# The odd table's rows loaded behind the last scatter, and the fifth tile's even rows added by a transfer, in a decoder layer with a mixture of experts

## The reference, cut to what matters

```
for each block of up to 128 routed rows of one expert:
    h = x[token rows];  y = (silu(h @ wg[e]) * (h @ wu[e])) @ wd[e]
routed[token] += y * gate                     # each token has 6 experts of 64
shared = (silu(x @ sh_wg) * (x @ sh_wu)) @ sh_wd
r = ALPHA * x + routed + shared
out = (r - mean(r)) * rsqrt(var(r) + eps) * g2 + b2
```

## Time and profile before

| | |
|---|---|
| time, median of three runs | 2006.88 us (2005.97 to 2007.66) |
| the profiled execution's own time | 2021.99 us |
| its span | 2019.8 us |
| TensorE busy | 1963.6 us, 97% of the span |
| VectorE, ScalarE, GpSimd busy | 67%, 46%, 30% |
| mean granted clock of TensorE | 0.988 of full speed |
| HBM read and written | 338.58 MB and 81.84 MB |

### The profile page before, as it was taken

One profiled execution on the slowest core, in us unless ns is written; L12 is line 12 of the kernel. 1 busy time (PEld: TensorE's weight loads), 2 busy tenths in 40 slices (PEclk: granted clock), 3 DMA queues, 4 the chain that ended last, 5 costly groups with the idle time before them and its releaser, 6 DMA issues. The chain is left out here.

```text
span 2019.8 us, 32329 instructions
## 1 busy us (share of the span) xinstructions
PE 1963.6 (97%) x9421; PEld 1479.3 (73%) x9422; DVE 1345.5 (67%) x2558; ACT 926.4 (46%) x1615; POOL 613.9 (30%) x403
## 2 busy tenths in 40 slices
PE   8999999999999999999999889999999999999996
PEld 7887787877768766668878637777777777777772
DVE  2794643444206677779867738887777877778876
ACT  2111221234212244550044237777777777677764
POOL 2433232323322220002143533333333333233331
PEclk9999999999999999989999899999999999999998
DMA  6122312132532210047671567999999999999986
GB/s 204 42 68 89 104 42 63 43 86 63 124 93 84 79 59 27 26 156 263 218 283 43 188 242 230 312 373 346 323 342 338 341 326 346 327 314 330 342 280 177
DMA packets 170898, 390.66 MB, mean 193 GB/s; under 512 B 27936, under 2 KB 100929, under 8 KB 146112
## 3 DMA queue, kind: packets, MB, share of 16 engines
q1 hardware_dynamic: 132032, 302.71, 41.5%
q0 software_dynamic: 29568, 70.09, 13.9%
q10 hardware_dynamic: 9216, 16.78, 2.2%
HBM read 338.58 MB, written 81.84 MB: 208 GB/s over the span
## 5 line engine op out<-in xcount | busy, mean ns | idle before, releaser
L660 PE MATMUL a_bank<-x_hi,w_hi 128*128 128x512 f32 x928 | 376.8, 406 | 0.0
L660 PE MATMUL a_bank<-x_hi,w_lo 128*128 128x512 f32 x928 | 363.4, 392 | 0.0
L660 PE MATMUL a_bank<-x_lo,w_hi 128*128 128x512 f32 x928 | 362.2, 390 | 0.0
L2382 DVE TENSOR_TENSOR u_lo<-w_gu,u_hi 128x1024 fp32r<-128x1024 f32 x225 | 268.4, 1221 | 37.0 <-ACT u_hi L2024 29.2
L2024 ACT ACTIVATE u_hi<-w_gu 128x1024 fp32r x225 | 230.5, 1065 | 17.5 <-SPq L1511 16.7
L594 POOL CAST w_hi<-w_raw 128x1024 fp32r<-128x1024 f32 x56 | 65.2, 1164 | 557.2 <-PE a_bank L660 557.2
L2397 DVE TENSOR_TENSOR d_lo<-w_d,d_hi 128x1024 fp32r<-128x1024 f32 x150 | 177.2, 1222 | 82.5 <-ACT d_hi L2132 81.4
L1814 PE MATMUL e_bank<-u_hi,x_g_hi 128*128 128x512 f32 x450 | 208.4, 463 | 0.0
L660 PEld LDWEIGHTS a_bank<-x_hi,w_hi 128*128 128x128 f32 x928 | 174.9, 188 | 39.4 <-issue 6.1
L660 PEld LDWEIGHTS a_bank<-x_hi,w_lo 128*128 128x128 f32 x928 | 174.5, 188 | 38.1
L660 PEld LDWEIGHTS a_bank<-x_lo,w_hi 128*128 128x128 f32 x928 | 175.3, 189 | 32.5 <-issue 0.5
(11 more groups left out here) (397 smaller groups left out, 3676.2 us busy)
## 6 DMA issues: line engine op xcount, KB each, us to landing
w_gu<-in_moe_wg SPq DMA_DIRECT2D x64, 1024.0 KB
w_gu<-in_moe_wu SPq DMA_DIRECT2D x64, 1024.0 KB
w_d<-in_moe_wd SPq DMA_DIRECT2D x64, 1024.0 KB, 25.5
w_raw<-in_w_in SPq DMA_DIRECT2D x53, 512.0 KB, 3.8
gates<-gate_out ACTq DMA_DIRECT2D x64, 256.0 KB, 2.0
g_sb<-gates SPq DMA_DIRECT2D x16, 1024.0 KB, 5.3
acc_odd<-zero POOLq DMA_DIRECT2D x9, 512.0 KB, 15.2
work<-in_w_out SPq DMA_DIRECT2D x4, 1024.0 KB, 7.8
```

The lines of the kernel that those rows point to most:

```text
L660: ins = pe.matmul(bank[h][:, :], w[:, c % 2, k, :], x[:, k, cols], start=(k == 0 and j == 0), stop=(k == KD - 1 and j == 2))
L2382: dve.tensor_tensor(up_part(u_lo[j]), up_weights(slot, j), up_part(u_hi[j]).bitcast(F32), ALU.subtract).then_inc(u_lo_dve, 1)
```

## The change

All odd blocks now go to `acc_odd`, block 2n-1 too; even blocks and the very last one, 2n+1, go to `acc`. `odd_whole` is given when block 2n-1 has landed, and by its place in POOL's stream only behind the issue of the last scatter. So all eight loads of odd rows stand behind that issue; three (tiles 4, 0, 5) before `rows_landed`, the others between the even rows, in the order in which the tail uses them. Tile 4's even rows are added by a POOL transfer like those of tiles 5 to 7 (order: 5, 4, 6, 7). VectorE's `total(4)` falls away; ScalarE makes tile 4's row sum and mean (`sum_of_four`). VectorE's `inverse(2, 4)` moves ahead of tile 5's sum, tile 5's sum ahead of tile 4's centering, and `center(6)` ahead of `inverse(4, 6)`.

```diff
@@ -1466,8 +1466,11 @@
         def odd_row(t):
             return x1_n[:, t, :] if t < NU else row_out(t)
 
-        def even_row(t):
-            return row_out(t) if t < NU else x1_n[:, t, :]
+        def summed_row(t):
+            return row_out(t) if t == NU else x1_n[:, t, :]
+
+        def normed_row(t):
+            return x1_n[:, t, :] if t == NU else row_out(t)
 
         DOWN_BANK = {NU: 2, NU + 1: 4, NU + 2: 2, NU + 3: 0}
 
...
@@ -1597,20 +1600,30 @@
                     sp.dma_start(tail_d, d['sh_wd'][0].rearrange('(k p) n -> p k n', p=P)).then_inc(tail_in, 16)
                     sp.dma_start(g2, d['ln2_g'].broadcast_to([P, D])).then_inc(ln_in2, 16)
                     sp.dma_start(b2, d['ln2_b'].broadcast_to([P, D])).then_inc(ln_in2, 16)
+            def odd_rows(t):
+                sp.dma_start(odd_row(t), acc_odd[t * P:(t + 1) * P, :]).then_inc(odd_in[t], 16)
+
+            def even_rows(t):
+                sp.dma_start(row_out(t), acc[t * P:(t + 1) * P, :]).then_inc(acc_row_in[t], 16)
             sp.wait_ge(odd_whole, 1)
             sp.wait_ge(d_blocks, blocks_until(E - 3) + 2)
-            for t in range(NU, NT):
-                sp.dma_start(odd_row(t), acc_odd[t * P:(t + 1) * P, :]).then_inc(odd_in[t], 16)
+            odd_rows(NU)
             sp.wait_ge(gu_blocks, blocks_until(E - 2) + 2)
-            for t in range(NU):
-                sp.dma_start(odd_row(t), acc_odd[t * P:(t + 1) * P, :]).then_inc(odd_in[t], 16)
+            odd_rows(0)
+            odd_rows(5)
             sp.wait_ge(gu_blocks, 2 * n + 4)
             sp.wait_ge(rows_landed, 1)
-            for t in range(NU + 1):
-                sp.dma_start(even_row(t), acc[t * P:(t + 1) * P, :]).then_inc(acc_row_in[t], 16)
+            even_rows(0)
+            odd_rows(1)
+            even_rows(1)
+            odd_rows(6)
+            for t in range(2, NU):
+                odd_rows(t)
+                even_rows(t)
+            odd_rows(7)
             for i, t in enumerate((0, 1, 4, 5, 6)):
                 sp.wait_ge(finished, i + 1)
-                sp.dma_start(out[0, t * P:(t + 1) * P, :], row_out(t)).then_inc(out_stored, 16)
+                sp.dma_start(out[0, t * P:(t + 1) * P, :], normed_row(t)).then_inc(out_stored, 16)
             for h in range(2):
                 cols = slice(h * HALF, (h + 1) * HALF)
                 sp.wait_ge(finished, h + 6)
...
@@ -1680,29 +1693,21 @@
             pool.wait_ge(acc_rest, 16 * (NT - NU))
             n = trips(pool)
 
-            def body(b, s, i, ahead=True, table=None, whole=False):
+            def body(b, s, i, ahead=True):
                 if ahead:
                     gather(s, b + 4)
-                if whole:
-                    pool.wait_ge(scattered[1], 16 * i + 16)
-                    pool.sem_inc(odd_whole, 1)
                 pool.wait_ge(y_act, b + 2)
                 pool.wait_ge(so_ready, b + 2)
                 pool.wait_ge(scattered[s], 16 * i + 16)
-                if table is not None:
-                    pool.wait_ge(scattered[1 - s], 16 * i + 32 - 16 * (1 - s))
                 pool.sem_inc(gathers, 1)
-                pool.indirect_dma_start(out=((acc, acc_odd)[s] if table is None else table)[:, :], out_offset=bass.IndirectOffsetOnAxis(ap=idx_out[:, s:s + 1], axis=0),
+                pool.indirect_dma_start(out=(acc, acc_odd)[s][:, :], out_offset=bass.IndirectOffsetOnAxis(ap=idx_out[:, s:s + 1], axis=0),
                                         in_=y_out[:, s, :], in_offset=None, bounds_check=S - 1, oob_is_err=False,
                                         compute_op=ALU.add
                                         ).then_inc(scattered[s], 16)
-            last = n - 1
-            with pool.Fori(0, last) as i:
+            with pool.Fori(0, n) as i:
                 for s in range(2):
                     body(2 * i + s, s, i)
-            body(2 * last, 0, last, whole=True)
-            body(2 * last + 1, 1, last, table=acc)
-            body(2 * n, 0, n, ahead=False, table=acc)
+            body(2 * n, 0, n, ahead=False)
             pool.wait_ge(y_act, 2 * n + 3)
             pool.wait_ge(so_ready, 2 * n + 3)
             pool.wait_ge(scattered[0], 16 * n + 32)
@@ -1710,16 +1715,19 @@
             pool.indirect_dma_start(out=acc[:, :], out_offset=bass.IndirectOffsetOnAxis(ap=idx_out[:, 1:2], axis=0),
                                     in_=y_out[:, 1, :], in_offset=None, bounds_check=S - 1, oob_is_err=False,
                                     compute_op=ALU.add).then_inc(scattered[0], 16)
+            pool.wait_ge(scattered[1], 16 * n + 16)
+            pool.sem_inc(odd_whole, 1)
             pool.wait_ge(scattered[0], 16 * n + 48)
-            pool.wait_ge(scattered[1], 16 * n + 16)
             pool.sem_inc(rows_landed, 1)
-            for t in range(NU + 1, NT):
+            for t in (5, 4, 6, 7):
+                if t == NU:
+                    pool.wait_ge(s_y, NU + 1)
                 pool.wait_ge(odd_in[t], 16)
-                pool.dma_start(out=odd_row(t), in_=acc[t * P:(t + 1) * P, :], accum_op=ALU.add).then_inc(even_in[t - NU - 1], 16)
+                pool.dma_start(out=odd_row(t), in_=acc[t * P:(t + 1) * P, :], accum_op=ALU.add).then_inc(even_in[t - NU], 16)
             pool.wait_ge(bias_out, 16 * len(ADDED))
             for i, t in enumerate(ADDED):
                 pool.wait_ge(scaled, i + 1)
-                pool.dma_start(out=out[0, t * P:(t + 1) * P, :], in_=row_out(t), accum_op=ALU.add).then_inc(out_added, 16)
+                pool.dma_start(out=out[0, t * P:(t + 1) * P, :], in_=normed_row(t), accum_op=ALU.add).then_inc(out_added, 16)
 
         @block.tensor
         def _(pe):
...
@@ -2179,12 +2187,23 @@
             copied(2 * n + 1, 1, n, 4)
             tail_gated(NU + 1)
 
+            def sum_of_four():
+
+                act.wait_ge(even_in[0], 16)
+                act.wait_ge(squared, 1)
+                act.activation(squares[:, 0, :], summed_row(NU), ACT.Copy, accum_out=row_sum[:, NU, 0:1]).then_inc(sum_four, 1)
+                act.wait_ge(sum_four, 1)
+                act.activation(neg_mean[:, NU:NU + 1], row_sum[:, NU, 0:1], ACT.Copy, scale=-1.0 / D).then_inc(mean_four, 1)
+
             def square(t):
 
-                act.wait_ge(mean_ready, t + 1)
+                if t == NU:
+                    act.wait_ge(mean_four, 1)
+                else:
+                    act.wait_ge(mean_ready, t + 1 - (t > NU))
                 if t >= 4:
                     act.wait_ge(squared, t - 3)
-                act.activation(squares[:, t % 4, :], x1_n[:, t, :], ACT.Square, bias=neg_mean[:, t:t + 1], accum_out=sq_sum[:, t:t + 1]
+                act.activation(squares[:, t % 4, :], summed_row(t), ACT.Square, bias=neg_mean[:, t:t + 1], accum_out=sq_sum[:, t:t + 1]
                                ).then_inc(squared, 1)
 
             def deviation(a, b):
...
@@ -2214,6 +2233,7 @@
             deviation(2, 4)
             act.wait_ge(s_down, NU + 2)
             tail_turned(7)
+            sum_of_four()
             normal(2)
             square(4)
             normal(3)
...
@@ -2496,8 +2516,11 @@
 
             def center(t):
 
-                dve.wait_ge(mean_ready, t + 1)
-                dve.scalar_tensor_tensor(row_out(t), x1_n[:, t, :], neg_mean[:, t:t + 1], g2, ALU.add, ALU.mult
+                if t == NU:
+                    dve.wait_ge(mean_four, 1)
+                else:
+                    dve.wait_ge(mean_ready, t + 1 - (t > NU))
+                dve.scalar_tensor_tensor(normed_row(t), summed_row(t), neg_mean[:, t:t + 1], g2, ALU.add, ALU.mult
                                          ).then_inc(centered, 1)
 
             def inverse(a, b):
...
@@ -2531,15 +2554,13 @@
             dve.wait_ge(s_ht, NU + 2)
             tail_hidden(7)
             final(1, slice(0, D))
-            dve.wait_ge(s_y, NU + 1)
-            total(4)
+            inverse(2, 4)
+            shared_total(5)
             center(4)
-            shared_total(5)
-            inverse(2, 4)
             center(5)
             shared_total(6)
+            center(6)
             inverse(4, 6)
-            center(6)
             final(4, slice(0, D))
             final(5, slice(0, D))
             shared_total(7)
```

More of the change, by code:

```diff
@@ L1439, in back @@
         scattered = [sem('scattered0'), sem('scattered1')]
-        even_in = [sem(f'even_in{t}') for t in range(NU + 1, NT)]
+        even_in = [sem(f'even_in{t}') for t in range(NU, NT)]
         odd_in = [sem(f'odd_in{t}') for t in range(NT)]
@@ L1458, in back @@
         ln_in2, sd_done2, out_added, out_stored = (sem(n) for n in ('ln_in2', 'sd_done2', 'out_added', 'out_stored'))
-        odd_whole, rows_landed, mean_ready, squared, half_down, finished = (
-            sem(n) for n in ('odd_whole', 'rows_landed', 'mean_ready', 'squared', 'half_down', 'finished'))
+        odd_whole, rows_landed, mean_ready, mean_four, sum_four, squared, half_down, finished = (
```

(5 more changed lines are left out.)

2 lines of the change are left out of this document (1 added, 1 removed).

## The result

The changed kernel takes 2010.14 us (median of 20 runs, 2004.63 to 2018.99), the kernel before beside it 2004.49 us (20 runs). Set against each other the ratio is 1.0028, with a 95% interval of 1.0018 to 1.0038: slower by 3.6 to 7.6 us. The likeliest case of the prediction had said 2.6 us more, which counts as no change; the sign was right, the size was half. Put on the prediction's base of 2006.9 us the ratio gives 2012.5 us: inside the stated range (to 2012.8), but above the forecast's own range (to 2011.5) and above the bound of 2010.9 from which the prediction counts as slower, a class to which it gave 0.21.

The account below looks back on a forecast made before the run. Limits one behind another: scatters until 1980 us, VectorE from 1984, DMA engines hidden beneath. total(3) at 1999.0 + 22.75 + 0.7 = 2022.4 against 2019.8, so 2.6 more: 2006.9 + 2.6 = 2009.5 us; range 2003.0 to 2012.8.

Parts of the forecast that it names:

- Block 2n's scatter 4.0 us earlier: Scatters: freed from waiting for block 2n-1's, block 2n's starts at 1966.3 instead of 1970.32 us.
- The last scatter at 2.71 us: End of the scatters: the last one starts at 1973.2 and lands at 1975.95 us, where it was 1979.97.
- the fourth rival: Scatters: block 2n's takes 8.75 us instead of 6.11, all behind is 2.6 later, 2012.1 us; chance 0.10.
- total(0) 1.2 us earlier: VectorE's first sum: tile 0's even rows, fourth in SP's queue, let it start at 1982.7 instead of 1983.93 us.
- total(3) 5.3 us later: VectorE's fourth sum waits for the eleventh load, sharing engines with accumulating tiles; starts at 1999.0 instead of 1993.68 us.
- upper bound of 2000.2: Load queue ahead of total(3): 6.9 tiles at the measured mixed rate of 1.97 us each take 13.6 us.
- The waits ahead of total(2) and total(3): VectorE waits for loads ahead of its third and fourth sums, together some 6 us.
- The first rival: Load queue: accumulating loads get little service, total(3) starts at 1992.45; 4.6 us less, 2002.3 us; chance 0.13.
- the third: Load queue: an accumulating tile costs no more than a plain one; 1.4 us less, 2005.5 us; chance 0.10.
- The rest of the tail, 22.75 + 0.7: From total(3) to the end: 26.1 less 1.5 and 2.5 plus 0.6 for new waits, and 0.7 for TensorE's clock.
- TensorE: Before the last matmuls it idles 5.1 us and its clock may halve, costing 0 to 1.3 us, taken as 0.7.
- the second rival: TensorE: tile 3's rows at 2000.2, clock at half through both tail_down; 4.9 us more, 2011.8 us; chance 0.15.

Follow-up runs that it names:

- e2: Changed kernel, but tile 4's even rows by a plain load, and tile 4's sum and VectorE's order as before; ratio 1.0027 to the kernel before.
- e5: Changed kernel with POOL's accumulating loads of tiles 5, 4 and 6 cut from 1024 columns to 16; one execution, tail 54.44 us, no ratio.
- e8: Changed kernel, but POOL issues its accumulating loads only when tile 3's even rows have landed; ratio 1.0013 to the kernel before.
- e3: Changed kernel, but the odd rows are loaded only when all scatters have landed; 2011.75 us, ratio 1.0034 to the kernel before.
- e1: Changed kernel with scatters and row loads put back as before, keeping tile 4's accumulation and the new VectorE and ScalarE order; ratio 0.9987 to the kernel before.
- e4: Changed kernel, but all eight odd loads are issued once block 2n-1's scatter has landed, ahead of the even ones; ratio 1.0009 to the kernel before.

## Why the prediction was partly right

Step by step, each against its own number:

- **Block 2n's scatter 4.0 us earlier: right.** It starts at T + 1.55 (predicted 1966.3 - 1964.85 = 1.45) and takes 5.91 us.
- **The last scatter at 2.71 us: wrong, and this is the step that failed.** The prediction had the first odd load issued at the end of the scatter's instruction, "1973.2 + 1.55 + 0.15", and so 1.7 us behind its start; it was 0.45 us. POOL's wait and increment behind an indirect DMA are evidently not held until that instruction, as the profile records it, ends; the same distance is 0.45 to 0.46 us in e2, e5 and e8. Three loads of 512 KB then ran beside the scatter, and it landed after 6.53 us. e3 has 2.70 without them. `rows_landed` came at T + 14.82 instead of 11.1, 0.3 us earlier than before, not 4.0. By the prediction's own sign ("last scatter landed about 1976, four before (else rival 4)") this was the fourth rival's case, though on another scatter and with 3.8 us instead of 2.6.
- **total(0) 1.2 us earlier: 0.5.** The loss was softened because the three odd tiles cost tile 0's even rows nothing any more: these landed 3.5 us after their issue at 1964.88, where the first load with nothing ahead of it had taken 3.7, although the second and third odd tile landed only at 1965.5 and 1966.8. `total(0)` was predicted at T + 17.85 and came at T + 18.61, only 0.8 us off. Two errors, a scatter too short by 3.8 us and a queue too long ahead of tile 0, nearly cancelled: that the forecast was near here is luck.
- **total(3) 5.3 us later: 7.3.** The mechanism, the sharing with accumulating tiles, is shown by e5 and e8. The term was mis-sized by 1.96 us (T + 34.15 predicted, 36.11 measured). 0.76 of it came with `total(0)`. The rest is in the queue: tile 3's even rows landed at 1968.46 + 17.5 = 1986.0, 17.5 us behind tile 0's at 1968.4, where the prediction has 16.1 (1982.6 to 1998.7), to which it had added 0.3 by taking 1999.0. In between seven plain and three accumulating tiles landed; by the rates that e8 shows (524 KB at 399 and 207 GB/s, 1.31 and 2.53 us) they are 16.8 us. So about half of the gap is the price of an accumulating tile, for which the prediction had 2.34 us, from a stretch that a little plain traffic had made faster. The other 0.7 us are not the price of mixing: at one packet each the two rates give 273 GB/s, and the mixed stretches had 273 and 276. Where they went is not shown. The upper bound of 2000.2 (T + 35.35) was the better guide than the sum of pure rates that I chose, and even it was passed: the measured place is 2001.0 on the prediction's clock, at the very edge of its sign of being wrong (after 2001).
- **The waits ahead of total(2) and total(3), "together some 6 us": 7.2** (5.90 + 1.30). The place was right. The first rival (no such wait) and the third (about 3 us) fall with it.
- **The rest of the tail, 22.75 + 0.7: right.** Measured 59.35 - 36.11 = 23.24. The 2.51 us wait became 0.20, tile 4's mean made nobody wait, and e1, with no gap in TensorE's work ahead of the last sixteen matmuls, has 51.77 - 28.73 = 23.04.
- **TensorE: right.** It idled 5.48 us (predicted 5.1). The earlier gap of 2.22 us and its 1.69 us of slower matmuls, which the prediction had not, delayed nobody. In the stretch from 1986 to 1989 the granted clock was 0.51 and from 1989 to 1991 0.50, the 1.2 GHz level; from 1991 to 1995 it was 0.76 on average:

```profile
1989.00:1991.00 2.00, 1.81 (x4) 1.15 (x5) 1.80 (x4) 1.99 (x4) 0.00 (x0) 0.50 1.02 152
1991.00:1995.00 4.00, 4.00 (x8) 1.62 (x7) 3.55 (x8) 3.97 (x7) 0.86 (x1) 0.76 0.61 186
```

  The last sixteen matmuls lost 1.61 us, of which 0.42 reached VectorE. So the clock's part of the second rival, at half through both `tail_down`, did not come: it needed 2 x 6.4 us and had 8.64. Its other part did: it has tile 3's rows at 2000.2 (T + 35.35), and they were later.

The sum: +7.28 at `total(3)`, -2.88 behind it (26.12 to 23.24), together +4.4 us of tail; predicted +5.3, -2.65, +2.6. The miss is the mis-sized queue. The predicted ratio was 2009.5 / 2006.9 = 1.0013, the measured interval begins at 1.0018. The ratio stands for 5.6 us, and the 1.2 us by which that exceeds the tail's 4.4 are not accounted for.

**A rule that bears on the failed step.** The last scatter was issued before the loads and landed after the first of them. The Trainium skill, page "DMA: Bandwidth & Descriptors", section "Queues, rings and completion order", has a DMA's semaphore increment as a strongly ordered write, which lands only after every earlier write of that DMA engine, whatever queue it came from. By that rule loads in SP's queue could hold back the landing of POOL's scatter. The trace doesn't show the 3.8 us there: the scatter landed 0.32 us after its own last packet had begun (1964.45 to 1964.77), as before the change (1979.64 to 1979.97, 0.33), and it was this packet that came late. That speaks for packets standing in turn behind those of the loads, and against increments held back.

e4 fits this. Its last scatter took 6.49 us though it began 4.9 us after the last of the odd loads had been issued (1948.81 + 5.61 = 1954.42 to 1959.29); but issued is not landed, and of the eight loads five landed while it ran and the last at 1966.1, behind its own landing at 1965.8.

What stays open: why eight loads cost a scatter 3.7 to 4.2 us (12.45 - 8.75, 10.11 - 5.91) and three cost 3.8 (6.53 - 2.70). Only one load landed while the changed kernel's last scatter ran (1961.9), and only one during block 2n's in e4 (1952.8), so the number issued says little. A kernel with one load beside the scatter would show whether there is a fixed part; it was not run. Nor was one that leaves out the scatter of a block without rows, some 3.5 us of the ladder before the change (0.8 from release to start, 2.71 to the landing).
